# Two transformer blocks on one core: the down product of the feed-forward parts as seven products per block instead of eight

## What is computed

```python
D_MODEL, SEQ, DEPTH, D_FF = 1024, 256, 2, 2816
ALPHA = (2.0 * DEPTH) ** 0.25

def _swiglu(x, wg, wu, wd):
    return (jax.nn.silu(x @ wg) * (x @ wu)) @ wd

for l in range(DEPTH):
    h = 0.5 * _swiglu(x, ffn_w_gate[l, 0], ffn_w_up[l, 0], ffn_w_down[l, 0])
    x = _layernorm(ALPHA * x + h, ln_g[l, 0], ln_b[l, 0])
    h = _mixer(x, ...)
    x = _layernorm(ALPHA * x + h, ln_g[l, 1], ln_b[l, 1])
    h = 0.5 * _swiglu(x, ffn_w_gate[l, 1], ffn_w_up[l, 1], ffn_w_down[l, 1])
    x = _layernorm(ALPHA * x + h, ln_g[l, 2], ln_b[l, 2])
```

## Time and profile before

| | |
|---|---|
| median of three runs | 2717.43 us (2715.28 to 2719.22) |
| profiled execution | 2721.32 us |
| its span, first to last instruction | 2719.5 us |
| mean granted TensorE clock | 0.989 |
| PE busy | 2630.4 us (97%) |
| DVE busy | 739.9 us (27%) |
| ACT busy | 442.0 us (16%) |
| FFN 0, its first product to the first of the mixer | 6.57 to 246.67 us |

### The profile page before, as it was taken

How to read it: one execution, slowest core, us unless ns; L and a number is a source line. 1 busy time by engine, 2 the same in 40 slices (tenths; PEclk the granted TensorE clock), 3 DMA queues, 4 the chain that set the end, 5 groups by cost and what they waited for, 6 DMA issues and landing times.

```text
span 2719.5 us, 41048 instructions
## 1 busy us (share of the span) xinstructions
PE 2630.4 (97%) x17415; PEld 1698.9 (62%) x17415; DVE 739.9 (27%) x1653; ACT 442.0 (16%) x852; POOL 11.5 (0%) x24
## 2 busy tenths in 40 slices
PE   9999999999999999999999998799998999989997
PEld 7777877777778877787778887433433334333432
DVE  1002610010006400035467665322222221212123
ACT  0001310010004200024332224111111110111111
POOL 0000000000000000000000000000000000000000
PEclk9999999999999999999999999799999999999999
DMA  8545154454445344462300104699999999999994
GB/s 290 180 154 199 66 203 153 153 195 148 153 154 200 130 151 153 154 242 99 117 25 4 49 4 172 253 420 420 420 419 415 420 420 414 392 415 420 420 391 187
DMA packets 91908, 637.41 MB, mean 234 GB/s; under 512 B 10664, under 2 KB 10664, under 8 KB 18304
## 3 DMA queue, kind: packets, MB, share of 16 engines
q1 hardware_dynamic: 90000, 628.62, 58.9%
q0 software_dynamic: 1744, 6.43, 1.0%
HBM read 632.38 MB, written 2.62 MB: 233 GB/s over the span
## 4 chain that ended last, share of the span: by engine, by line
PE 57%; issue 40%; DVE 2%; ACT 1%; DMA 0%; DVEq 0%; POOLq 0%; POOL 0%; SPq 0%
PE ps L657 22%; PE ps L668 11%; PE ps L864 6%; PE ps L755 4%; PE ps L815 2%; PE ps L1113 1%; PE ps L1124 1%; PE ps L1129 1%; PE ps L727 1%; PE ps L635 1%; PE ps L900 1%; PE ps L911 1%; PE ps L1025 0%; PE ps L1061 0%; PE ps L737 0%
## 5 line engine op out<-in xcount | busy, mean ns | idle before, releaser
L657 PE MATMUL ps<-X,ring 128*128 128x256 f32 x2816 | 617.9, 380 | 7.2 <-DMA ring<-weights 6.6
L657 PEld LDWEIGHTS ps<-X,ring 128*128 128x128 f32 x2816 | 536.1, 191 | 96.4 <-issue 25.3
L1300 PE MATMUL ps<-arena 128*64 128x512 f32 (+1 forms) x1224 | 352.0, 602 | 10.0 <-issue 10.0
L1300 PE MATMUL ps<-ring,arena 128*64 128x512 f32 (+1 forms) x1248 | 335.3, 596 | 1.3 <-ACT arena L1756 1.3
L668 PE MATMUL ps<-ring,arena 128*128 128x512 f32 x704 | 308.6, 592 | 0.0
L1838 DVE TENSOR_TENSOR arena<-ps,arena 128x512 f32<-128x512 f32 x44 | 30.4, 692 | 820.4 <-PE ps L657 813.0
L1300 PEld LDWEIGHTS ps<-arena 128*64 128x64 f32 (+1 forms) x1224 | 123.6, 145 | 178.5 <-issue 173.8
L668 PEld LDWEIGHTS ps<-ring,arena 128*128 128x128 f32 x704 | 133.8, 190 | 151.3 <-issue 149.2
L1300 PEld LDWEIGHTS ps<-ring,arena 128*64 128x64 f32 (+1 forms) x1248 | 110.0, 140 | 178.8 <-issue 175.2
L864 PE MATMUL ps<-arena,ring 128*128 128x256 f32 x784 | 173.0, 380 | 0.0
L864 PEld LDWEIGHTS ps<-arena,ring 128*128 128x128 f32 x784 | 147.7, 190 | 25.0 <-issue 5.6
(11 more groups left out here) (477 smaller groups left out, 2472.7 us busy)
## 6 DMA issues: line engine op xcount, KB each, us to landing
ring<-weights SPq DMA_DIRECT2D x366, 1024.0 KB, 6.9
arena<-weights SPq DMA_DIRECT2D x153, 1024.0 KB, 16.6
con<-weights SPq DMA_DIRECT2D x25, 1024.0 KB, 16.2
vec<-weights SPq DMA_DIRECT2D x25, 1024.0 KB, 15.6
vec<-weights SPq DMA_DIRECT2D x25, 512.0 KB, 13.8
con<-weights SPq DMA_DIRECT2D x25, 512.0 KB, 15.6
con<-consts SPq DMA_DIRECT2D x1, 1872.5 KB, 13.8
vec<-vectors SPq DMA_DIRECT2D x1, 1671.5 KB, 16.8
```

The source lines that it names most:

```text
L657: last = mm(dst[:, f, :], w[:, k, f * P:(f + 1) * P], X[:, k, :], start=(k == 0), stop=(k == KD - 1))
L1300: last = mm(put(half), stationary(4 * kq + k), part[:, at:at + 512], start=False, stop=(kq == 1 and k == 3))
```

## The change

The down product of a chunk is a product of 2x2 pieces: two token halves x two halves of the chunk, times two halves of the chunk x two halves of the model columns. It is now made with seven products of 128x512 instead of eight (`down`), in Strassen's way, from pieces and sums of pieces.

- **Fifteen sums in all.** Four are of the weights (`WS`, 128x512 each, `weight_sums`), and four are of the hidden values (`HS`, 128x128 each, `hidden_sums`), all on DVE and per chunk. The seven joining sums are made once per FFN (`ffn_ln`), since the seven products M1 to M7 are summed up over all chunks, each in a bank of its own (`M_BANK`). The residual goes into M2, M3, M7 and M4. For the last, DVE makes `XR`, a difference of tiles of `X`.
- **Half chunks.** Seven banks are taken, so gate and up have one bank (4) left. `gate_up` makes half a chunk (gate and up of one `f`), then PE does four of the seven products of the chunk before (part 0), then the second half chunk, then the other three (part 1). ACT and DVE take each half chunk by itself (`silu`, `hidden`, 128x256). Each half of gate and up waits until bank 4 has been read. A chunk's gate and up blocks are both released in its second half.
- **Place of the sums.** The weight sums of chunk J stand on DVE between the hidden products of its first and its second half. They wait for the load of its down block, which the products before needed a chunk later. `decay_and_bias` and `context_norm` now stand behind the weight sums of chunk 1 and ahead of the hidden product of its second half.
- **The join.** ACT copies M1 and M7 out of PSUM (`P1K`, `P7K`), DVE makes the sums for the first token half and one quarter of the second, PE adds two sums to M4 by products with the identity, and ACT writes the normed rows of the first token half.
- Some semaphores are folded into the step counters. The mixer's norm (`mixer_ln`) is as before.

```diff
+        M_BANK = {1: 7, 2: 0, 3: 1, 4: 3, 5: 5, 6: 6, 7: 2}
...
+                def gate_up(slot, turns, H, f, entry=None, early=False):
+                    if H is not None:
+                        pe.wait_ge(hidden_ready, H)
+                    dst = ps[:, 5 if early else 4, :].rearrange("p (w t) -> p w t", w=2)
                     for which in range(2):
                         s = (slot + which) % RING
-                        if m != 0 or which:
+                        if f == 0 and (entry != 0 or which):
                             pe.wait_ge(slot_loaded[s], turns[which])
...
+                        for k in range(KD):
+                            if entry == 0 and which == 0 and f == 0 and k % 4 == 0:
+                                pe.wait_ge(x_loaded, 16 * (k // 4 + 1))
+                                pe.wait_ge((first_half, slot_loaded[0])[k // 4], 16)
+                            if entry is not None and which == 0 and f == 0:
+                                x_column(entry, k)
+                            last = mm(dst[:, which, :], w[:, k, f * P:(f + 1) * P], X[:, k, :], start=(k == 0), stop=(k == KD - 1))
+                        if f:
+                            last.then_inc(block_used, 1)
+                    if f == 0:
+                        last.then_inc(gate_half, 1)
+
+                def down(slot, turn_, J, S, buf, part, begins=False, ends=False):
+                    h = [HF[:, buf, f, t * P:(t + 1) * P] for t in range(2) for f in range(2)]
+                    s = [HS[:, buf, i * P:(i + 1) * P] for i in range(4)]
+                    w = ring[:, slot % RING, :].rearrange("p (q n) -> p q n", q=4)
+                    t = [WS[:, buf, i, :] for i in range(4)]
+                    table = ((1, h[0], w[:, 0, :]), (2, h[1], w[:, 2, :]), (6, s[1], t[2]), (5, s[0], t[0]),
+                             (3, s[3], w[:, 3, :]), (7, s[2], t[1]), (4, h[3], t[3]))
+                    for which, left, right in table[:4] if part == 0 else table[4:]:
+                        if which == 1:
+                            pe.wait_ge(slot_loaded[slot % RING], turn_)
+                            pe.wait_ge(hidden_ready, J * 2 + 3)
+                        if which == 6:
+                            pe.wait_ge(sums_ready, S)
+                        last = mm(ps[:, M_BANK[which], :], left, right, start=begins and which in (1, 5, 6), stop=False, skip_group_check=True)
+                        if which == 4:
+                            last.then_inc(block_used, 1)
+                        elif ends:
+                            last.then_inc(m_summed, 1)
+                    if part and ends:
+                        pe.wait_ge(sum_part, 4 * FCH * (n + 1) + 2 * n + 1)
+                        mm(ps[:, M_BANK[4], :], ident, US, start=False, stop=False, skip_group_check=True)
+                        pe.wait_ge(m_kept, 2 * n + 2)
+                        mm(ps[:, M_BANK[4], :], ident, P7K, start=False, stop=False, skip_group_check=True).then_inc(m_summed, 1)
...
+                def chunk(j, b, J, S, h, loop=None):
+                    add = 0 if loop is None else loop * 16
+                    gate_up(b, [add + turn(b), add + turn(b + 1)], J * 2 + 1, 0)
+                    down(b + 2, add + turn(b + 2), J - 1, S, (J0 + j + 1) % 2, 0, j == 1)
+                    gate_up(b, None, J * 2 + 2, 1)
+                    down(b + 2, None, None, None, (J0 + j + 1) % 2, 1)
+
+                gate_up(base, [turn(base), turn(base + 1)], 2 * J0 + 1 if n else None, 0, m)
+                gate_up(base, None, None, 1, early=True)
...
-                residual(0, range(2))
+                for which, cols in ((2, [X[:, k, 0:P] for k in range(4)]), (3, [X[:, 4 + k, 0:P] for k in range(4)]),
+                                    (7, [X[:, 4 + k, P:2 * P] for k in range(4)]), (4, [XR[:, k, :] for k in range(4)])):
+                    if which == 4:
+                        pe.wait_ge(sums_ready, n * (FCH + 1) + 1)
+                    for k in range(4):
+                        mm(ps[:, M_BANK[which], k * P:(k + 1) * P], cols[k], RES[:, 0, :], start=(k == 0), stop=False, skip_group_check=True)
...
+                S0 = n * (FCH + 1) + 2
+                for j in (1, 2):
+                    chunk(j, base + 3 * j - 1, J0 + j, S0 + j - 1, j)
+                with pe.Fori(0, (FCH - 3) // 2) as i:
                     for h in range(2):
-                        b = base + 2 + 3 * h
-                        chunk_gate_up(b, [i * 16 + turn(b), i * 16 + turn(b + 1)], i * 2 + (J0 + 1 + h), (J0 + 1 + h) % 2)
-                        chunk_down(b + 2, i * 16 + turn(b + 2), i * 2 + (J0 + 1 + h), (J0 + h) % 2)
-                chunk_down(base + 2 + 3 * (FCH - 1), turn(base + 2 + 3 * (FCH - 1)), J0 + FCH, (J0 + FCH - 1) % 2, True)
+                        j = 3 + h
+                        chunk(j, base + 3 * j - 1, i * 2 + (J0 + j), i * 2 + (S0 + j - 1), h, i)
+                last = base + FFN_BLOCKS - 1
+                for part in range(2):
+                    down(last, turn(last), J0 + FCH - 1, S0 + FCH - 1, (J0 + FCH - 1) % 2, part, False, True)
...
+                def silu(J, f, used, early=False):
+                    if f == 0:
+                        act.wait_ge(gate_half, J + 1)
+                    else:
+                        act.wait_ge(block_used, used)
+                    if not (isinstance(J, int) and J == 0):
+                        act.wait_ge(hidden_ready, J * 2 + f)
...
+                for which, count, kept in ((1, 1, P1K), (7, 6, P7K)):
+                    act.wait_ge(m_summed, 7 * n + count)
+                    A(kept, ps[:, M_BANK[which], :], ACT.Copy).then_inc(m_kept, 1)
...
+                if m % 3 != 1:
+                    i = m - (m + 1) // 3
+                    act.wait_ge(sum_part, 4 * FCH * (i + 1) + 2 * i + 2)
+                    for h in range(2):
+                        part = XH[:, 0, h * 512:(h + 1) * 512]
+                        A(part, part, ACT.Identity, scale=RD[:, 0:1], bias=NB[:, 0:1]).then_inc(xh_ready, 1)
...
+                def hidden(J, f, buf, early=False):
+                    dve.wait_ge(silu_ready, J * 2 + f + 1)
+                    v.tensor_tensor(HF[:, buf, f, :], ps[:, 5 if early else 4, T:2 * T], SG[:, f, 0, :], ALU.mult).then_inc(hidden_ready, 1)
+
+                def weight_sums(J, buf, slot, turn):
+                    w = ring[:, slot % RING, :].rearrange("p (q n) -> p q n", q=4)
+                    dve.wait_ge(slot_loaded[slot % RING], turn)
+                    v.tensor_tensor(WS[:, buf, 0, :], w[:, 1, :], w[:, 0, :], ALU.subtract)
+                    v.tensor_tensor(WS[:, buf, 1, :], w[:, 3, :], w[:, 1, :], ALU.subtract).then_inc(sum_part, 1)
+                    dve.wait_ge(sum_part, J * 4 + 2 * n + 1)
+                    v.tensor_tensor(WS[:, buf, 2, :], w[:, 3, :], WS[:, buf, 0, :], ALU.subtract).then_inc(sum_part, 1)
+                    dve.wait_ge(sum_part, J * 4 + 2 * n + 2)
+                    v.tensor_tensor(WS[:, buf, 3, :], w[:, 2, :], WS[:, buf, 2, :], ALU.subtract)
+
+                def hidden_sums(J, buf):
+                    h, s = HF[:, buf, :, :], HS[:, buf, :].rearrange("p (q t) -> p q t", q=4)
+                    dve.wait_ge(hidden_ready, J * 2 + 3)
+                    v.tensor_tensor(s[:, 0, :], h[:, 0, P:2 * P], h[:, 1, P:2 * P], ALU.add).then_inc(sum_part, 1)
+                    v.tensor_tensor(s[:, 2, :], h[:, 0, 0:P], h[:, 0, P:2 * P], ALU.subtract)
+                    dve.wait_ge(sum_part, J * 4 + 2 * n + 3)
+                    v.tensor_tensor(s[:, 1, :], s[:, 0, :], h[:, 0, 0:P], ALU.subtract).then_inc(sum_part, 1)
+                    dve.wait_ge(sum_part, J * 4 + 2 * n + 4)
+                    v.tensor_tensor(s[:, 3, :], h[:, 1, 0:P], s[:, 1, :], ALU.subtract).then_inc(sums_ready, 1)
...
+                v.tensor_tensor(XR[:, :, :], X[:, 0:4, P:2 * P], X[:, 4:8, P:2 * P], ALU.subtract).then_inc(sums_ready, 1)
+                hidden(J0, 0, J0 % 2)
+                hidden(J0, 1, J0 % 2, True)
+                if n == 0:
+                    dve.wait_ge(pe_step, PE_STEP["rel_ready"])
+                    v.tensor_scalar(RV[0:HEADS, P:2 * P], ps[0:HEADS, 7, 0:P], 8.0, None, ALU.mult).then_inc(dve_step, 1)
+                weight_sums(J0, J0 % 2, *down_block(0))
+                hidden_sums(J0, J0 % 2)
+                for j in (1, 2):
+                    hidden(J0 + j, 0, (J0 + j) % 2)
+                    weight_sums(J0 + j, (J0 + j) % 2, *down_block(j))
+                    if j == 1 and n == 0:
+                        decay_and_bias()
+                    if j == 1 and n == 3:
+                        context_norm()
+                    hidden(J0 + j, 1, (J0 + j) % 2)
+                    hidden_sums(J0 + j, (J0 + j) % 2)
...
+            def ffn_ln(m, used):
+                i = m - (m + 1) // 3
+                M = [None] + [ps[:, M_BANK[q], :] for q in range(1, 8)]
```

(26 more changed lines are left out.)

188 lines of the change are left out of this document (91 added, 97 removed).

## The result

The changed kernel takes **2694.57 us** (median of four runs, 2694.09 to 2697.31) against 2718.32 of the kernel before in the same session (2715.28 to 2719.60). The ratio is 0.991, with a 95% interval from 0.9899 to 0.9922. The forecast was 2694.5 in a range from 2687 to 2706. The profiled execution of the changed kernel took 2694.47 us, 26.8 less than the one of before.

A forecast was written before the change was run, and what follows sets the result against it. PE's products alone were taken to bound the FFNs. Terms -34.4 + 7.8 + 3.4 + 0.2 = -22.9 us gave 2698.4 against the profiled execution, which lay 3.9 above the median: 2694.5 us expected, range 2687 to 2706.

The forecast's parts named there:

- Products removed, -34.4: Down products of 40 chunks: eight become seven at 0.859 us each, 34.4 us less, chunks lasting 19.82 us.
- The bank handshake, 0: Gate and up halves waiting for bank 4: about 1.2 us, hidden behind PE's products, so no cost.
- Rival (a): Half chunks: the bank wait bites partly, at 0.25 us each 10 us over 40 second halves, 2704 us; chance 0.13.
- DVE's sums in steady chunks, 0: Steady chunks: sums and hidden products take 5.3 of 19.8 us on DVE, covered by PE's products; no cost.
- rival (d): Every chunk: DVE waits for down blocks landing after 16.4 us; gain gone from 17.0, 2934 us at worst; chance 0.05.
- FFN 0, 3.4: FFN 0, chunk 1: DVE waits for a late down block, then sums, chain and hidden product; PE loses 3.4 us.
- just inside 16.4: FFN 0, chunk 2: down block lands 15.5 us after the chunk's new start, within the 16.4 us allowed; no wait.
- FFN 3, 0.2: FFN 3, chunk 1: `context_norm` behind the weight sums makes the hidden product seen at 20.0 against 19.8; 0.2 us more.
- The join, 4 x 1.95: End of each FFN: joining sums and root's table load delay the narrow products by 1.95 us, four times, 7.8 us.
- Rival (c): The join: links overlap so only PE's extra product counts, -4.4 us, 2690 us; chance 0.04.
- Rival (b): The join: a drain of 1.38 us with each table load, 5.5 us in all, 2700 us; chance 0.05.
- The expert stage, 0: Expert stage behind the FFNs, code left alone by the change: forecast difference 0 from the last mark to the end.

The follow-up runs named there:

- experiment 7: The changed kernel with the seven products split six and one instead of four and three, leaving less cover for the bank handshake; 2715.27 us in one run.
- experiment 4: The changed kernel with the table write on GpSimd's queue held back until the eleventh hidden product is ready; 2692.97 us in one run.
- experiment 5: The changed kernel with one unused 128x1 root on ACT behind each FFN's last silu, so the root's table loads early; 2693.52 us, ratio 0.9904.
- experiment 3: The changed kernel with the decay chain on DVE in FFN 0 moved from chunk 1 to behind chunk 2's weight sums; 2697.59 us in one run.

## Why the prediction held, and where it didn't

- **Products removed, -34.4: right.** 40 products at 0.859; chunks 19.82 apart.
- **The bank handshake, 0: right.** 1.26 us against 1.2, measured by experiment 7; cover 2.58. Rival (a) fell.
- **DVE's sums in steady chunks, 0: right**, and rival (d) fell there. But it was the true danger of the change: its condition, a landing later than 16.4 us into the chunk, was met by chunk 2's block in the changed kernel, and by a later block in experiment 4, and PE waited both times.
- **FFN 0, 3.4: too small by 3.0.** The wait that it prices came by the mechanism forecast (late block, sums, chain, hidden product), at 2.0 us, since the block landed at 40.5 instead of 41.6 and sums and chain took 7.8 us instead of 8.15. Two steps failed. One took the landing of chunk 2's block from the kernel before, 65.9, which is 15.5 us after the new start and "just inside 16.4". The block was issued 1.0 us sooner and landed 2.2 us later, at 68.1. It took 21.0 to 21.5 us in all seven traces of changed code with the write at this place, and 17.6 to 17.9 in the four of the kernel before, with and without copies. The step left out that the change also moves the two loads ahead of it, since a chunk's gate and up blocks are both freed in its second half: the three are issued at 40.95, 44.41 and 46.98, where before they were spread over 14 us (34.25, 41.16, 48.02). That this is why the block took longer isn't tested by itself. The other is a cost that the sum didn't have: after the wait PE came back at half clock, 1.7 us here.
- **FFN 3, 0.2: right** (0.1, from its 6.2 us against 6.3 of FFN 1).
- **The join, 4 x 1.95: mis-sized, 4 x 2.30 measured.** The mechanism was right (the table load is in the path, experiment 5), and so are nearly all its links, counted from 231.68: the copy starts at 5.34 (5.35 forecast), the load ends at 7.24 (7.25), ACT's normed halves start at 7.98 (7.95). The one that failed is their length: 1.52 us, where the step has 1.15 (7.95 to 9.1). That is 0.37, the whole of what is missing. Rival (c), a quicker join, fell.
- **Rival (b), a drain at the table load: fell**, here as in the earlier trace rows: 238.93 follows on 237.64 + 1.28. The Trainium skill's 1.38 us (page "ScalarE: Activation LUTs", section "What ACT_TABLE_LOAD costs") are in no row of either kernel.
- **The expert stage, 0: wrong, by 7.4 us in the traces.** That a change leaves some code alone doesn't keep its time: its place in the engine's code moved. Another 0.7 came from the stretch ahead of it. Together they outweigh the 4.2 us that the FFNs lacked: the changed kernel's trace is 3.9 us below the 2698.4 that the sum gives for it. That the median came out at 2694.57 against a forecast of 2694.5 is luck; the FFNs alone, with the stages behind them unchanged, would have given about 2699 (an estimate, 2717.4 - 18.7).

## What to carry to other kernels

When work is put on an idle engine, look at what it is queued ahead of, not at its sum: the sums had 14 us to spare in each chunk and cost 6 us all the same, because the one product that PE needed stood behind a load. Put what somebody waits for first; that order alone was worth 6.4 us in FFN 0. A wait of a busy TensorE is to be priced with the half clock that can follow it, and a kernel with a runtime loop can gain or lose some us by nothing but the place of that loop. Before a few us of the whole time are put down to an edit, look in each trace at how long PE stood at half clock in stages that the edit doesn't touch.

## What was not expected of the hardware

- The granted clock fell to 0.50 after waits as short as 2.0 us. From the end of one product to the start of the next, PE stood idle for 2.7 us ahead of chunk 3 of the changed kernel, and 32 passes then took 8.6 us instead of 6.9; after 4.5 us (experiment 4) they took 8.7, after 4.2 (experiment 3) 9.6. 2.0 us ahead of chunk 2 cost no clock in the changed kernel (7.0 us for the 32 passes) and 1.8 us in experiment 5, whose row is below: the same wait has either outcome.

```profile
48.95 8.86 PE L670 MATMUL ps<-X,ring 128*128 128x256 f32 x32 [1.87 <-DVE arena L1892]
```

- One write of 1.5 MB took 36 to 39 us, and 1 MB loads issued while it ran and at least 15 us before its end landed after 18 to 22 us instead of 4.8 (one that was issued 0.9 us behind the write's start took 6.2). It did so at both places where it was put.
- Outside the change, the time of one and the same stretch of 500 us differed by 5.4 us between executions, in step with the time that PE stood at half clock in it.
- A turn of the runtime loop costs PE 1.8 to 2.3 us and, by the place of the loop in the code, 0, 3.2 to 3.5, or 4.6 to 5.2 us more some 5 us later. Each of the second waits ended in a stretch at half clock or was followed by one within 1 us; of the eight turns without one, two had such a stretch.
